# Six of 192 expert-weight loads cut into seven transfers of unequal row counts

## What is computed

```python
logits = (xt @ w_router).astype(jnp.float32) + b_router.astype(jnp.float32)
top_v, top_i = lax.top_k(logits, TOP_K)          # TOP_K = 4 of N_EXPERTS = 32
gates = jax.nn.softmax(top_v, axis=-1)
...
hdn = xb @ w_gate_up[e] + b_gate_up[e]           # w_gate_up: 32 x 1024 x 2048
return clamped_swiglu(hdn) @ w_down[e] + b_down[e]  # w_down: 32 x 1024 x 1024
```

## Time and profile before

| | us |
|---|---|
| median of 3 runs | 1699.66 (1698.82 to 1702.07) |
| profiled execution | 1699.34 |
| its span | 1697.5 |
| TensorE matmul busy | 1467.5 (86%) |
| VectorE busy | 757.7 (45%) |
| ScalarE busy | 465.0 (27%) |
| DMA | 549.32 MB, mean 324 GB/s |

### The profile page before, as it was taken

One profiled execution on the slowest core, in us unless ns is written; L12 is line 12 of the kernel. 1 busy time (PEld: TensorE's weight loads), 2 busy tenths in 40 slices (PEclk: granted clock), 3 DMA queues, 4 the chain that ended last, 5 costly groups with the idle time before them and its releaser, 6 DMA issues. The chain is left out here.

```text
span 1697.5 us, 26362 instructions
## 1 busy us (share of the span) xinstructions
PE 1467.5 (86%) x10245; PEld 850.2 (50%) x10245; DVE 757.7 (45%) x1439; ACT 465.0 (27%) x888; POOL 34.2 (2%) x54
## 2 busy tenths in 40 slices
PE   5999888886898998689876656769999999999998
PEld 4977522332232332123321111138888877988886
DVE  3686425241324322134231322247774556756664
ACT  3435310000000001000000000036553536565543
POOL 2201000000000000000000000000000000000000
PEclk9999999999999999789999987789999999999999
DMA  9878899999999999999999999973464722514460
GB/s 366 321 299 321 357 425 426 425 425 425 425 426 425 427 412 417 425 426 428 424 426 426 426 424 426 424 278 123 166 257 173 312 101 100 199 42 173 178 241 25
DMA packets 70066, 549.32 MB, mean 324 GB/s; under 512 B 6033, under 2 KB 8858, under 8 KB 45306
## 3 DMA queue, kind: packets, MB, share of 16 engines
q1 hardware_dynamic: 67832, 543.05, 77.8%
q0 software_dynamic: 1744, 3.53, 0.6%
q10 hardware_dynamic: 306, 0.12, 0.0%
HBM read 545.61 MB, written 1.07 MB: 322 GB/s over the span
## 5 line engine op out<-in xcount | busy, mean ns | idle before, releaser
L1397 PE MATMUL PS<-ring,arena 128*32 128x512 f32 x2512 | 319.5, 646 | 82.2 <-DMA ring<-in_w_gate_up 76.6
L1689 DVE TENSOR_TENSOR weights_low<-ring,weights_high 128x1024 fp32r<-128x1024 f32 x212 | 257.8, 1220 | 95.7 <-ACT weights_high L752 95.5
L1083 PE MATMUL PS<-ht_pair,weights_high 128*128 128x512 f32 x832 | 294.3, 398 | 3.9 <-DVE weights_low L1689 2.6
L752 ACT ACTIVATE weights_high<-ring 128x1024 fp32r<-128x1024 f32 x212 | 222.8, 1056 | 104.3 <-PE PS L1079 100.3
L752 ACT ACTIVATE arena<-PS 128x256 f32<-128x256 f32 (+2 forms) x237 | 100.6, 432 | 509.6 <-PE PS L1462 332.4
L2080 DVE TENSOR_SCALAR arena<-PS 128x256 f32<-128x256 f32 x47 | 19.9, 424 | 485.1 <-PE PS L1397 485.1
L1085 PE MATMUL PS<-ht_pair,weights_low 128*128 128x256 f32 x832 | 233.8, 281 | 0.0
L1397 PEld LDWEIGHTS PS<-ring,arena 128*32 128x32 f32 x2512 | 80.8, 114 | 295.3 <-issue 174.5
L1462 PE MATMUL PS<-ring,arena 128*32 128x512 f32 x1504 | 168.8, 594 | 17.3 <-PEq L509 10.9
L1083 PEld LDWEIGHTS PS<-ht_pair,weights_high 128*128 128x128 f32 x832 | 156.9, 189 | 42.2 <-issue 4.8
L752 ACT ACTIVATE arena<-arena 128x256 f32<-128x256 f32 (+2 forms) x113 | 45.7, 405 | 455.1 <-DVE arena L2080 454.4
(11 more groups left out here) (291 smaller groups left out, 1577.5 us busy)
## 6 DMA issues: line engine op xcount, KB each, us to landing
ring<-in_w_gate_up SPq DMA_DIRECT2D x106, 2048.0 KB, 33.6
ring<-in_w_down SPq DMA_DIRECT2D x64, 2048.0 KB, 35.2
arena<-in_w_gate_up SPq DMA_DIRECT2D x22, 2048.0 KB, 35.4
ring<-in_w_in SPq DMA_DIRECT2D x6, 4096.0 KB, 13.3
ring<-in_w_ada SPq DMA_DIRECT2D x5, 4096.0 KB, 16.9
ring<-in_ffn_wg SPq DMA_DIRECT2D x4, 4096.0 KB, 13.7
ring<-in_ffn_wu SPq DMA_DIRECT2D x4, 4096.0 KB, 13.3
ring<-in_ffn_wd SPq DMA_DIRECT2D x4, 4096.0 KB, 13.5
```

The lines of the kernel that those rows point to most:

```text
L752: return nc.scalar.activation(out_, in_, func, **kw)
L1083: mm(PS[:, bank, :].rearrange("p (a t) -> p a t", a=2), high, HT_PAIR[:, :, k, :], start=first, stop=False, skip_group_check=True)
L1397: ins = mm(PS[CH * t:CH * (t + 1), c % INL, :].rearrange("p (u n) -> p u n", u=2), XTE[b][c % INL][:, KT // 2 * half + k, :], w[:, k % 2, ...
L1689: v.tensor_tensor(low, w, high, ALU.subtract).then_inc(sem("split_low"), 1)
```

## The change

`cuts(u)` gives the row ranges in which part u is loaded. For u = 31, 63, 95, 127, 159 and 191 there are seven: partitions 0 to 63, 64 to 95, 96 to 102, 103 to 109, 110 to 116, 117 to 123 and 124 to 127. For all other parts it is one range of 128, as before. SyncE issues the seven one after the other behind the one wait, each with its increment of 16, and the counts for which TensorE and the later slabs wait are raised to match.

```diff
+CUTS = ((0, 64), (64, 96), (96, 103), (103, 110), (110, 117), (117, 124), (124, 128))
...
+        def cuts(u):
+
+            return CUTS if u % 32 == 31 else ((0, P),)
...
-                uses = [n + len([u for u in range(6 * NE) if place_of(u) == 2 * k]) for k, n in enumerate(uses)]
+                uses = [n + sum(len(cuts(u)) for u in range(6 * NE) if place_of(u) == 2 * k) for k, n in enumerate(uses)]
...
-            uses_here = len([v for v in range(u + 1) if place_of(v) == place])
+            uses_here = sum(len(cuts(v)) for v in range(u + 1) if place_of(v) == place)
...
-                sp.dma_start(*expert_part(u % 6, u // 6, place)).then_inc(part_full[place], 16)
+                dst, src = expert_part(u % 6, u // 6, place)
+                for p0, p1 in cuts(u):
+                    sp.dma_start(dst[p0:p1], src[p0:p1]).then_inc(part_full[place], 16)
```

## The result

| | us |
|---|---|
| before, on the same chip | 1700.87 (1698.82 to 1702.53, 4 runs) |
| changed | 1810.99 (1809.85 to 1817.2, 4 runs) |
| ratio | 1.0655, 95% interval 1.0639 to 1.0672 |
| span before, after | 1697.5, 1809.4 |

The changed kernel is 110 us slower. The direction was the one forecast; the size was not: +42 was predicted, and the range ended at 1762.

The account below looks back on a forecast made before the run. The full DMA engines were taken to bound the expert stage. The balance gain and the crowding, in one estimate of +42 us (middle of +15 to +69), on 1699.3 gave 1741, or 1742 against the median; range 1691 to 1762.

Parts of the forecast that it names:

- What bounds the kernel: Expert stage: DMA engines full at about 425 GB/s, TensorE has slack; the last part's landing ends it at 1123.4 us.
- issue: SyncE's six more instructions per cut part: 2.0 us, hidden behind some 34 us of queue; cost nothing, 12 us at most.
- Rows by engine: In a cut part four engines get 11 rows, three 10, nine 6, instead of 8; the stage ends 7.4 us earlier.
- If the nine laggards are those nine: The nine engines ending the expert stage last are those with 6 rows per cut part; they lose 7.4 us.
- the lead of 20 us: Seven engines end the expert stage about 20 us ahead of the last; subtracted from the cost for the seven.
- rival 2: No crowding, but the seven early engines are not the lowest: a laggard gets 11 rows, 11 us later, 1711; chance 0.06.
- Time of a row: Cut transfers write few neighbouring partitions, so rows hold their engines longer: +15 to +69 us with lanes, taken as +42.
- lanes: The way into on-chip memory has 16 lanes; 64 or 32 neighbouring partitions meet in eight, each row taking twice as long.
- the upper end: Every meeting at its worst: 14.8 us more per cut part, 89 for six, less the 20 us lead: 69 us later.
- The 1.40: In the b_down loads, a byte to 32 partitions held its engine 1.40 times as long; as whole effect, 7 us later.
- the instruction packets: In the DMA queues, 87 packets of 16 KB, 92 us of engine time, 11.5 us each over eight engines, delay nine engines.

Follow-up runs that it names:

- columns: Changed kernel with its seven transfers per cut part split by columns, each over all 128 partitions: 1701.42 us, +0.1 against the kernel before, ratio 1.0001.
- rows_apart: Kernel before, loading only 64 rows of each of the six parts, in eight transfers of eight neighbouring source rows to partitions four apart: 1699.94 us, ratio 0.9997.
- rows_together: Kernel before, loading only 64 rows of each of the six parts, in eight transfers of source rows four apart to neighbouring partitions: 1751.20 us, ratio 1.0293.
- halves: Changed kernel with the six parts cut into two transfers, partitions 0 to 63 and 64 to 127: 1774.01 us, +72.7 against the kernel before, ratio 1.0426.
- cut_late: Changed kernel with the seven transfers for part 159 alone: 1718.63 us, +18.4 against the kernel before, ratio 1.0106.
- cut_early: Changed kernel with the seven transfers for part 31 alone: 1711.91 us, +11.7 against the kernel before, ratio 1.0063.
- striped: Changed kernel with the same seven transfer sizes, but partitions taken with strides so none are neighbours: 1734.59 us, +33.6 against the kernel before, ratio 1.0206.
- halves_mixed: Changed kernel with the six parts cut into two transfers of 64 rows, even and odd partitions: 1701.60 us, +1.4 against the kernel before, ratio 1.0009.
- extra_one: Kernel before with five additional memory-to-memory copies of one 16 KB row behind each of the six parts: 1701.38 us, +1.2, ratio 1.0012.

## Why the prediction was wrong

*What bounds the kernel* was right: the loss in the stage (112.1 us) is the loss in the span (111.9), and issue and number of transfers cost nothing, also by `columns`.

*Rows by engine*: the spreading 11, 10, 6 was right by the count of packets. The step that failed is "If the nine laggards are those nine", and with it the lead of 20 us that I took off every estimate for the seven. The seven early engines are not the seven lowest: of the lowest seven, four are early, two in the middle and one is the last of all. The last one is among those with three rows more for each cut, so the balance alone is worth +11.1 us and not -7.4, and rival 2 (+11, at a chance of 0.06) had this half of the mechanism. The profile of before shows how many engines are late, not which; the prediction said so in the rival and still subtracted the lead in the sum. Nor are there nine laggards that end together. The share of 0.56 from 1119 to 1123 us was read as nine engines at the last part; by its increments eight of them had finished it between 1116.7 and 1118.3 us and were at the next load, and one alone ended the stage.

*Time of a row*: the second step that failed is the size of this term. The mechanism was right, by destination (`rows_apart` against `rows_together`) and by lanes (213 to 219 GB/s at a full share). For the transfers of 64 and 32 rows I had 2.5 us a cut for engines with 6 rows, which makes 4.9 for engines with 8; `halves` measured 72.7 / 6 = 12.1. The transfers of seven and four rows were to bring an engine from those 4.9 to 14.8 us, 9.9 more a cut. They add 110 - 73 = 37 us in all, 6.2 us a cut, of which the 3 rows more on the last engine are 1.9. So the large transfers cost the most and the small ones less than I thought. My reason to go below the upper end, that drifting engines meet less, went against the runs: `cut_late`, where they are further apart, costs more than `cut_early`.

*The upper end* of 69 us was called the worst, and the result lies 41 us above it: 20 of them are the lead that I took off and that was not there. The other 21 are 6 x (12.1 - 4.9) = 43 us more for the large transfers and 6 x (9.9 - 6.2) = 22 less for the small. That the large ones cost so much I put down to the drift, which is argued and not measured by itself.

*The 1.40* from one us of small loads was too short a stretch: `halves` shows 425 / 217 = 1.96.

What stays open: why the rate of all 16 engines halves for some 12 to 20 us, where a cut part holds 4.9 us of rows at full rate. That engines in whole parts are held up in a half lane by those in the cut, while the other half of the lanes idles, fits the half rate and the drift, but no run follows a single engine. Why the last engine is late stays open too; that the instruction packets keep nine engines back was argued in the prediction, and no run tests it. Nor was it measured why the rate dips in `striped` where no neighbours are left, and not in `halves_mixed`.

## What to carry to other kernels

A transfer that shares the queues with others should spread over the partitions as they do: two of 64 neighbours cost 12 us each time where even and odd partitions cost nothing. When rows are to be moved between DMA engines, first find which engine is the last, with copies that touch nothing else, and count their packets, to see over how many engines they really went; that seven are early does not say that the lowest seven are. And where all queues are full, price a disturbance by the time until all engines have passed it, not by its own rows.

## What was not expected of the hardware

With full queues, cuts into neighbouring halves brought the rate to 213 to 219 GB/s for all transfers in flight, at a DMA share of 1.01 to 1.03: the busy share cannot show the crowding, only GB/s can. In the kernel before one DMA engine ended the stage 5.1 us after the next and 19.7 us after the first, and it is one of the lowest four, by the copies of four rows. A copy of one row of 16 KB from memory to memory went over all 16 engines in pieces of 1 KB, by 16 + 16 packets for each copy in `extra_one`, where copies of four rows went over four engines.
